# Prompt attention of a two-layer decoder step: alternating the order of TensorE's work between even and odd steps

## The chip, the cores and the metric

The program runs on one core of one Trainium2 chip. Its time is the device time of one execution in microseconds (us), as a median of several runs. The engines of the core work from queues of their own and wait for each other on semaphores: TensorE (PE in the profile, its weight loads PEld), VectorE (DVE), ScalarE (ACT), GpSimd (POOL) and SyncE (SP, which starts transfers).

## What is computed

One inference step of a two-layer decoder: 512 prompt tokens and 8 sample tokens, width 1024, 16 heads of 64 in 4 key/value groups. Layer 0 mixes tokens with native sparse attention (NSA), layer 1 with indexer sparse attention (DSA); each layer has a SwiGLU before and behind its mixer. The part that matters here is prompt attention, in blocks of 128 queries:

```python
# NSA: the selected and the window branch are softmax attention over the tokens
s = jnp.einsum('btkgd,btkmd->btkgm', qr, ks).astype(jnp.float32) * scale
p = masked_softmax(s, smask[:, :, :, None, :])
o_slc = jnp.einsum('btkgm,btkmd->btkgd', p.astype(vs.dtype), vs)
...
return g[..., 0:1] * o_cmp + g[..., 1:2] * o_slc + g[..., 2:3] * o_win
...
# DSA: one branch, over the tokens that the indexer chose
p = masked_softmax(s, valid[:, :, None, None, :])
return jnp.einsum('btkgm,btmkd->btkgd', p.astype(v.dtype), v)
```

All of it is in float32.

## The kernel before

The function attention() runs twice: once for layer 0 (names that begin with nsa_att, two branches and a compressed part) and once for layer 1 (dsa_att, one branch). It works on pairs of heads. A pair in one branch is a round, s = 0, 1, ...: 16 rounds in NSA, 8 in DSA. A round has four steps, one for each block of 128 queries, i = 0 to 3; the steps are numbered through, m = 4s + i. Block i looks at (i+1) x 128 keys. A step goes through these stations:

1. scores(m), on PE, L963: two matmuls on 64 rows each, into one of two banks s_ps (the bank of step m-2, so it waits for max_done of step m-2).
2. maximum(m), on DVE, L1087: adds the mask, finds the row maximum and writes probs; for each of the two heads.
3. exp(m), on ACT, L1044.
4. weigh(m), on DVE, L1093: the reciprocal of the sums. Then POOL, L950, scales probs by it.
5. turn(m), on PE, L981: transposes of 128x128 into one of two banks t_ps: 2 of them for i = 0, 4 for i = 1, 6 for i = 2 (two groups of 3), 8 for i = 3 (two groups of 4). A group waits until the group two before it has been copied out of its bank.
6. copy, out of t_ps into probs_t: on DVE, L1106, for i = 0, 2 and 3; on ACT, L1053, for i = 1.
7. values(s, kc), on PE, L1008, four of them in a round, in the round after it (the last in the one after that). In NSA compressed_values, L998, comes once in two rounds.
8. output, when a pair of heads is done: half on DVE, L1111, half on ACT, L1060.

The order on each engine is written out by loops over m. On PE a step takes scores(m+2), then turn(m-1), then the values that are due. On DVE a step takes weigh(m), maximum(m+2), then a side job if there is one, then the copy of step m-1 (none when i = 2), then the output if one is due (i = 1). On ACT a step takes exp(m+2), then (i = 2) the copy, or (i = 1) the output. Each engine takes its list in this order. The side job is there in DSA alone, in steps 4 to 20: one VectorE instruction in a step (L2536, L2538 in turns, L2534 at the end) that chooses keys for the sample tokens.

Below, S128, S256, S384 and S512 are the scores of i = 0 to 3; T2, T4, T6 and T8 the turns of i = 0 to 3; V with its widths the values, and C the compressed values. In these words PE's order in a round before is: S384 T8 V256, S512 T2 (C), S128 T4 V512, S256 T6 V384+V128.

Of the kernel before, what the change touches and what calls it, by code (L numbers as in the profile page):

```python
# [168 lines left out]
def warm_up(e, pe, out, count):  # L169


    for _ in range(count):
        pe.matmul(out, e.ident_b[:, :], e.causal_b[:, :], start=True, stop=True)
# [698 lines left out]
def attention(e, name, qt, branches, compressed, ot, prefetch, aside=None, prepare=None):  # L872
# [6 lines left out]
    nb = len(branches)  # L879
    S = 8 * nb  # L880
    M = 4 * S
    PT = 2560
    with ExitStack() as ctx:
# [21 lines left out]
        def groups_of(i):  # L905
            return ((0, (0, 1)),) if i == 0 else ((1, (0, 1)),) if i == 1 else ((2 * i - 2, (0,)), (2 * i - 1, (1,)))
# [5 lines left out]
        def block_at(i, kc, par):  # L912

            return kc * P if par == 0 else (i - kc) * P
# [7 lines left out]
        def moving(s, kc, par):  # L922
            at = 384 * kc if par == 0 else 2048 - 512 * kc
            return probs_t[s % 2][:, at + P * kc:at + 512]

        @block.sync
        def _(sp):
            prefetch(sp)
# [24 lines left out]
        @block.tensor  # L953
        def _(pe):
            def scores(m):
                i, b, p = m % 4, m // 4 % nb, m // (4 * nb)
                width, bank = (i + 1) * P, s_ps[m % 2]
                if m >= 2:

                    max_done.wait(pe, 2 * m - 2)  # L960
                for par in range(2):
                    rows = slice(par * HD, (par + 1) * HD)
                    mm = pe.matmul(bank[:, par, 0:width], qt[rows, p, i * P:(i + 1) * P], branches[b].kt[rows, p // 4, 0:width],  # L963
                                   start=True, stop=True)
                mm.then_inc(s_ready.sem, 1)

            def turn(m):
                s, i = m // 4, m % 4
                for g, pars in groups_of(i):
                    if 6 * s + g >= 2:  # L970

                        if g == 3:
                            act_copied.wait(pe, s + 1)
                        else:
                            dve_copied.wait(pe, 5 * s + (-1, 0, 1, 0, 2, 3)[g])
                    scaled.wait(pe, 2 * m + pars[-1] + 1)
                    for par in pars:
                        at = par * (i + 1) * P if len(pars) == 2 else 0
                        for kc in range(i + 1):
                            to = at + block_at(i, kc, par)  # L980
                            mm = pe.transpose(t_ps[g % 2][:, to:to + P], probs[i][par][:, kc * P:(kc + 1) * P], e.ident[:, :])  # L981
                    mm.then_inc(t_ready.sem, 1)

            def o_free(s):
                p = s // nb
                if p >= 2:

                    o_act.wait(pe, p - 1)
                    o_dve.wait(pe, p - 1)

            def compressed_values(s):

                p = s // nb
                p_t, v_bd = compressed
                o_free(s)
                for par in range(2):
                    head = 8 * (p // 4) + 4 * par + p % 4
                    pe.matmul(o_ps[p % 2][par * HD:(par + 1) * HD, :], v_bd[:, head, :], p_t, start=True, stop=False)  # L998

            def values(s, kc):  # L1000
                p, b = s // nb, s % nb
                if kc == 0:
                    act_copied.wait(pe, s + 1)
                    dve_copied.wait(pe, 5 * s + 5)
                    if b == 0 and compressed is None:
                        o_free(s)
                for par in range(2):
                    mm = pe.matmul(o_ps[p % 2][par * HD:(par + 1) * HD, kc * P:512],  # L1008
                                   branches[b].v_of(kc, 2 * (p // 4) + par), moving(s, kc, par),
                                   start=kc == 0 and b == 0 and compressed is None, stop=b == nb - 1 and kc == 2)  # L1010
                if kc == 2:
                    mm.then_inc(pv_done.sem, 1)

            warm_up(e, pe, o_ps[0][:, 0:P], 64)
            scores(0)
            scores(1)
            for m in range(M + 1):
                s, i = m // 4, m % 4
                if m + 2 < M:
                    scores(m + 2)  # L1020
                if m >= 1:
                    turn(m - 1)
                if m >= 5:
                    if i == 1 and (s - 1) % nb == 0 and compressed is not None:
                        compressed_values(s - 1)
                    if i == 2:
                        values(s - 1, 0)
                    if i == 3:
                        values(s - 1, 1)
                        values(s - 1, 3)  # L1030
                if i == 0 and s >= 2:
                    values(s - 2, 2)
            if compressed is not None and (S - 1) % nb == 0:
                compressed_values(S - 1)
            for kc in (0, 1, 3, 2):
                values(S - 1, kc)
# [1786 lines left out]
```

## Time and profile before

| | before |
|---|---|
| median of 3 runs | 2402.17 us (2398.2 to 2403.61) |
| the profiled execution | 2401.8 us, span 2400.0 us |
| busy PE / DVE / ACT / POOL | 95% / 45% / 31% / 14% of the span |
| NSA prompt attention | first scores at 679.25 us, last values done at 827.07 us |
| DSA prompt attention | first scores at 1834.14 us, last values done at 1912.47 us |

The times of the last two lines are read from the timeline of PE. A busy share is of the whole span; the two attention stages are 226 us of it together, and their shares are read by windows. In the timeline, a row gives the start, the duration, the engine, the line and operation, and in brackets how long the engine was idle before it and which engine's work ended that. In float32 each matmul of L963, L1008 and L998 shows as two entries, so "x4" there is two matmuls; a transpose shows as one.

### The profile page before, as it was taken

The page shows a single profiled execution, that of the slowest core. Times are in us where ns is not written, and L with a number is a line of the kernel's source. Part 1 is how long each engine was busy: PE and PEld are TensorE (multiplying, and loading weights), DVE is VectorE, ACT ScalarE, POOL GpSimd, SP SyncE. Part 2 cuts the span into 40 slices and gives each one's busy share as a digit, 9 for nine tenths or more (in the row PEclk, how much of TensorE's full clock was granted, in tenths as well). Part 3 has the DMA queues.
Part 4 walks back from the last instruction along what each step waited for, and adds up shares of the span by engine and source line. Part 5 has one row for each costly group of instructions (what it writes and reads, how often), then busy time and mean ns, then how long its engine had stood idle before and what let it go on. Part 6 is the DMA issues. An engine that isn't in the chain of part 4 may idle for free. (4 is left out here: it accounts for less than half of the span.)

```text
span 2400.0 us, 42964 instructions
## 1 busy us (share of the span) xinstructions
PE 2278.6 (95%) x17146; PEld 2057.5 (86%) x17146; DVE 1081.9 (45%) x1907; ACT 737.5 (31%) x1224; POOL 334.2 (14%) x422
## 2 busy tenths in 40 slices
PE   5999999996899999999999999999998889999997
PEld 5999999775764479999999999999665479999997
DVE  5442443223267644433434442444376735433433
ACT  2221332223146533322222221322255523322221
POOL 1000003100135321000012000003174320000002
PEclk8999999997999999999999999999999989999998
DMA  3332332224430022333232333332213022232331
GB/s 99 96 101 81 90 97 78 82 79 125 159 115 1 27 68 84 95 97 88 87 102 75 95 96 88 89 100 71 79 53 109 1 70 79 88 105 79 87 101 58
DMA packets 328119, 202.53 MB, mean 84 GB/s; under 512 B 11698, under 2 KB 307946, under 8 KB 327962
## 3 DMA queue, kind: packets, MB, share of 16 engines
q1 hardware_dynamic: 323866, 199.19, 27.9%
q10 hardware_dynamic: 4160, 2.10, 0.3%
q8 instruction: 59, 0.97, 0.2%
q14 instruction: 34, 0.28, 0.0%
HBM read 194.74 MB, written 10.70 MB: 86 GB/s over the span
## 5 line engine op out<-in xcount | busy, mean ns | idle before, releaser
L159 DVE TENSOR_TENSOR w_lo<-w_stage,w_hi 128x1024 fp32r<-128x1024 f32 (+1 forms) x268 | 356.4, 1330 | 827.1 <-ACT w_hi L152 827.0
L152 ACT ACTIVATE w_hi<-w_stage 128x1024 fp32r<-128x1024 f32 (+1 forms) x278 | 314.0, 1130 | 751.0 <-PE y_ps L166 344.2
L164 PE MATMUL gate_ps<-h_hi,w_hi 128*128 128x260 f32 x1408 | 402.3, 286 | 17.2 <-DVE h_lo L188 7.5
L165 PE MATMUL gate_ps<-h_lo,w_hi 128*128 128x260 f32 x1408 | 401.1, 285 | 0.0
L166 PE MATMUL gate_ps<-h_hi,w_lo 128*128 128x260 f32 x1408 | 400.3, 284 | 0.0
L164 PE MATMUL up_ps<-h_hi,w_hi 128*128 128x260 f32 x1408 | 398.8, 283 | 0.0
L164 PE MATMUL y_ps<-a_hi,w_hi 128*128 128x260 f32 x1408 | 398.5, 283 | 0.0
L165 PE MATMUL up_ps<-h_lo,w_hi 128*128 128x260 f32 x1408 | 398.1, 283 | 0.0
L165 PE MATMUL y_ps<-a_lo,w_hi 128*128 128x260 f32 x1408 | 398.0, 283 | 0.0
L166 PE MATMUL y_ps<-a_hi,w_lo 128*128 128x260 f32 x1408 | 397.9, 283 | 0.0
L166 PE MATMUL up_ps<-h_hi,w_lo 128*128 128x260 f32 x1408 | 397.4, 282 | 0.0
L164 PEld LDWEIGHTS gate_ps<-h_hi,w_hi 128*128 128x128 f32 x1408 | 268.1, 190 | 19.6 <-issue 15.8
L206 POOL TENSOR_TENSOR sq<-x 128x520 f32<-128x520 f32 x48 | 55.9, 1165 | 1561.6 <-DVE x L446 1110.6
L165 PEld LDWEIGHTS gate_ps<-h_lo,w_hi 128*128 128x128 f32 x1408 | 268.8, 191 | 0.0
L166 PEld LDWEIGHTS gate_ps<-h_hi,w_lo 128*128 128x128 f32 x1408 | 268.8, 191 | 0.0
L165 PEld LDWEIGHTS up_ps<-h_lo,w_hi 128*128 128x128 f32 x1408 | 265.7, 189 | 0.1
L166 PEld LDWEIGHTS up_ps<-h_hi,w_lo 128*128 128x128 f32 x1408 | 265.8, 189 | 0.0
L164 PEld LDWEIGHTS y_ps<-a_hi,w_hi 128*128 128x128 f32 x1408 | 265.6, 189 | 0.0
L166 PEld LDWEIGHTS y_ps<-a_hi,w_lo 128*128 128x128 f32 x1408 | 265.2, 188 | 0.0
L165 PEld LDWEIGHTS y_ps<-a_lo,w_hi 128*128 128x128 f32 x1408 | 265.2, 188 | 0.0
L164 PEld LDWEIGHTS up_ps<-h_hi,w_hi 128*128 128x128 f32 x1408 | 264.9, 188 | 0.1
L364 ACT ACTIVATE a_hi<-act_t 128x520 f32 (+1 forms) x88 | 56.3, 639 | 241.2 <-DVE act_t L427 241.2
(420 smaller groups left out, 3142.4 us busy)
## 6 DMA issues: line engine op xcount, KB each, us to landing
w_stage<-w_ffn_in SPq DMA_DIRECT2D x176, 512.0 KB, 3.7
w_stage<-w_ffn_out SPq DMA_DIRECT2D x64, 704.0 KB, 4.5
w_stage<-w_nsa_in SPq DMA_DIRECT2D x20, 512.0 KB, 3.4
w_stage<-w_dsa_in SPq DMA_DIRECT2D x16, 512.0 KB, 3.6
w_stage<-w_nsa_out SPq DMA_DIRECT2D x8, 512.0 KB, 3.6
cmp_page<-cache_nsa_cmp SPq DMA_DIRECT2D x16, 256.0 KB, 4.3
w_stage<-w_dsa_out SPq DMA_DIRECT2D x8, 512.0 KB, 3.7
nsa_win_s<-state_nsa_win SPq DMA_DIRECT2D x1, 4080.0 KB
```

The lines of the kernel that those rows point to most:

```text
L152: act.activation(e.w_hi[slot][:, 0:cols], e.w_stage[slot][:, 0:cols], ACT.Copy).then_inc(e.hi_done, 1)
L159: dve.tensor_tensor(e.w_lo[slot][:, 0:cols], e.w_stage[slot][:, 0:cols], e.w_hi[slot][:, 0:cols].bitcast(F32), ALU.subtract).then_inc(e.lo ...
L164: pe.matmul(out, w_hi, x_hi, start=first, stop=False)
L165: pe.matmul(out, w_hi, x_lo, start=False, stop=False)
L166: return pe.matmul(out, w_lo, x_hi, start=False, stop=last)
L206: pool.tensor_tensor(e.sq[:, :], e.x[:, i, :], e.x[:, i, :], ALU.mult).then_inc(e.sq_done, 1)
L364: act.activation(a_hi[:, j, :] if isinstance(j, int) else a_hi[:, ds(j, 1), :], act_t[:, :, :], ACT.Copy).then_inc(e.a_hi_done, 1)
```

## The change

The diff touches the loop of PE in attention() alone. In even steps the order stays: scores, turn, values. In odd steps it becomes values, turn, scores. Nothing is added or taken away; no other engine's list is touched, and all waits stay with the instructions that had them.

```diff
             for m in range(M + 1):
                 s, i = m // 4, m % 4
-                if m + 2 < M:
-                    scores(m + 2)
-                if m >= 1:
-                    turn(m - 1)
-                if m >= 5:
-                    if i == 1 and (s - 1) % nb == 0 and compressed is not None:
+                if i % 2 == 0:
+
+                    if m + 2 < M:
+                        scores(m + 2)
+                    if m >= 1:
+                        turn(m - 1)
+                    if i == 2 and s >= 1:
+                        values(s - 1, 0)
+                    if i == 0 and s >= 2:
+                        values(s - 2, 2)
+                else:
+
+                    if i == 1 and s >= 1 and (s - 1) % nb == 0 and compressed is not None:
                         compressed_values(s - 1)
-                    if i == 2:
-                        values(s - 1, 0)
-                    if i == 3:
+                    if i == 3 and s >= 1:
                         values(s - 1, 1)
                         values(s - 1, 3)
-                if i == 0 and s >= 2:
-                    values(s - 2, 2)
+                    turn(m - 1)
+                    if m + 2 < M:
+                        scores(m + 2)
```

PE's list in a round of NSA without compressed values, before, from S384 on (nsa_att_s_ps are scores, nsa_att_t_ps turns, nsa_att_o_ps values):

```order
L963 MATMUL nsa_att_s_ps<-nsa_kt,nsa_qt 128x384 x2
L981 MATMUL nsa_att_t_ps<-const,nsa_att_p 128x128 x8
L1008 MATMUL nsa_att_o_ps<-nsa_att_pt,nsa_z 64x256 x2
L963 MATMUL nsa_att_s_ps<-nsa_kt,nsa_qt 128x512 x2
L981 MATMUL nsa_att_t_ps<-const,nsa_att_p 128x128 x2
L963 MATMUL nsa_att_s_ps<-nsa_kt,nsa_qt 128x128 x2
L981 MATMUL nsa_att_t_ps<-const,nsa_att_p 128x128 x4
L1008 MATMUL nsa_att_o_ps<-nsa_att_pt,nsa_z 64x512 x2
L963 MATMUL nsa_att_s_ps<-nsa_kt,nsa_qt 128x256 x2
L981 MATMUL nsa_att_t_ps<-const,nsa_att_p 128x128 x6
L1008 MATMUL nsa_att_o_ps<-nsa_att_pt,nsa_z 64x384 x2
L1008 MATMUL nsa_att_o_ps<-nsa_att_pt,nsa_z 64x128 x2
```

And PE's list in the same round now:

```order
L963 MATMUL nsa_att_s_ps<-nsa_kt,nsa_qt 128x384 x2
L981 MATMUL nsa_att_t_ps<-const,nsa_att_p 128x128 x8
L1008 MATMUL nsa_att_o_ps<-nsa_att_pt,nsa_z 64x256 x2
L981 MATMUL nsa_att_t_ps<-const,nsa_att_p 128x128 x2
L963 MATMUL nsa_att_s_ps<-nsa_kt,nsa_qt 128x512 x2
L963 MATMUL nsa_att_s_ps<-nsa_kt,nsa_qt 128x128 x2
L981 MATMUL nsa_att_t_ps<-const,nsa_att_p 128x128 x4
L1008 MATMUL nsa_att_o_ps<-nsa_att_pt,nsa_z 64x512 x2
L1008 MATMUL nsa_att_o_ps<-nsa_att_pt,nsa_z 64x384 x2
L1008 MATMUL nsa_att_o_ps<-nsa_att_pt,nsa_z 64x128 x2
L981 MATMUL nsa_att_t_ps<-const,nsa_att_p 128x128 x6
L963 MATMUL nsa_att_s_ps<-nsa_kt,nsa_qt 128x256 x2
```

S512 has moved behind T2 and next to S128; S256 has moved behind T6, to the end of the round and next to the following S384; the values of the fourth step stand next to V512. Neighbours of one kind are more, changes of kind fewer.

PE's list in DSA with its waits, before, around S256 and T6 (dsa_att_s_ps are scores, dsa_att_t_ps turns):

```order
L963 MATMUL dsa_att_s_ps<-dsa_kt,dsa_qt 128x256 [waits max_done]
L963 MATMUL dsa_att_s_ps<-dsa_kt,dsa_qt 128x256
L981 MATMUL dsa_att_t_ps<-const,dsa_att_p 128x128 [waits probs_scaled,dve_copied]
L981 MATMUL dsa_att_t_ps<-const,dsa_att_p 128x128 x2
L981 MATMUL dsa_att_t_ps<-const,dsa_att_p 128x128 [waits probs_scaled,act_copied]
L981 MATMUL dsa_att_t_ps<-const,dsa_att_p 128x128 x2
L1008 MATMUL dsa_att_o_ps<-dsa_att_pt,dsa_z 64x384 x2
L1008 MATMUL dsa_att_o_ps<-dsa_att_pt,dsa_z 64x128 x2
```

And PE's list now, in the same place:

```order
L1008 MATMUL dsa_att_o_ps<-dsa_att_pt,dsa_z 64x384 x2
L1008 MATMUL dsa_att_o_ps<-dsa_att_pt,dsa_z 64x128 x2
L981 MATMUL dsa_att_t_ps<-const,dsa_att_p 128x128 [waits probs_scaled,dve_copied]
L981 MATMUL dsa_att_t_ps<-const,dsa_att_p 128x128 x2
L981 MATMUL dsa_att_t_ps<-const,dsa_att_p 128x128 [waits probs_scaled,act_copied]
L981 MATMUL dsa_att_t_ps<-const,dsa_att_p 128x128 x2
L963 MATMUL dsa_att_s_ps<-dsa_kt,dsa_qt 128x256 [waits max_done]
L963 MATMUL dsa_att_s_ps<-dsa_kt,dsa_qt 128x256
```

S256 now stands behind both groups of T6, the second of which waits for ACT's copy (act_copied).

## Rows read from the trace of the kernel before

**Rows 1.** Windows: start and end, us, busy PE, PEld, DVE, ACT, POOL, clock, DMA.

```profile
740.00:760.00 20.00, 19.76 (x124) 9.49 (x119) 14.86 (x63) 11.29 (x39) 10.42 (x19) 1.00 0.01 2
...
1866.00:1876.00 10.00, 8.69 (x56) 4.18 (x52) 8.74 (x37) 5.85 (x21) 4.12 (x8) 1.00 0.00 0
```

**Rows 2.** Timeline of all engines in NSA: start, duration, engine, line, operation.

```profile
745.80 0.69 DVE L1111 COPY nsa_ot<-nsa_att_o_ps 64x512 f32<-64x512 f32 x1
...
746.65 0.29 DVE L1087 CUSTOM_DVE_ANT_0 nsa_att_p<-nsa_att_s_ps,nsa_att_diagonal 128x128 f32<-128x128 f32 x1
...
746.99 0.40 ACT L1044 ACTIVATE nsa_att_p<-nsa_att_p,nsa_att_neg_max 128x128 f32<-128x128 f32 x1
...
747.40 0.70 PE L963 MATMUL nsa_att_s_ps<-nsa_kt,nsa_qt 64*128 64x256 f32 x4
...
747.77 0.63 ACT L1053 ACTIVATE nsa_att_pt<-nsa_att_t_ps 128x256 f32<-128x256 f32 x2
...
748.15 0.42 DVE L1087 CUSTOM_DVE_ANT_0 nsa_att_p<-nsa_att_s_ps,nsa_att_diagonal 128x256 f32<-128x256 f32 x1 [0.85 <-PE nsa_att_s_ps L963]
...
748.85 1.01 DVE L1106 COPY nsa_att_pt<-nsa_att_t_ps 128x384 f32<-128x384 f32 x2
...
749.78 0.21 DVE L1093 RECIPROCAL nsa_att_weight<-nsa_att_sums 128x1 f32<-128x1 f32 x2
...
749.95 0.92 PE L963 MATMUL nsa_att_s_ps<-nsa_kt,nsa_qt 64*128 64x384 f32 x4
...
750.79 1.09 PE L981 MATMUL nsa_att_t_ps<-const,nsa_att_p 128*128 128x128 f32 x8
750.91 0.56 DVE L1087 CUSTOM_DVE_ANT_0 nsa_att_p<-nsa_att_s_ps,nsa_att_diagonal 128x384 f32<-128x384 f32 x1 [0.92 <-PE nsa_att_s_ps L963]
...
751.82 0.65 PE L1008 MATMUL nsa_att_o_ps<-nsa_att_pt,nsa_z 128*64 128x256 f32 x4
...
751.87 1.28 DVE L1106 COPY nsa_att_pt<-nsa_att_t_ps 128x512 f32<-128x512 f32 x2
...
752.40 1.13 PE L963 MATMUL nsa_att_s_ps<-nsa_kt,nsa_qt 64*128 64x512 f32 x4
...
753.33 1.09 POOL L950 TENSOR_SCALAR nsa_att_p<-nsa_att_p,nsa_att_weight,nsa_gates 128x256 f32<-128x256 f32 x2 [2.42 <-DVE nsa_att_weight L1093]
...
753.46 0.44 PE L981 MATMUL nsa_att_t_ps<-const,nsa_att_p 128*128 128x128 f32 x2
753.58 0.69 DVE L1087 CUSTOM_DVE_ANT_0 nsa_att_p<-nsa_att_s_ps,nsa_att_diagonal 128x512 f32<-128x512 f32 x1 [0.29 <-PE nsa_att_s_ps L963]
...
753.83 0.49 PE L963 MATMUL nsa_att_s_ps<-nsa_kt,nsa_qt 64*128 64x128 f32 x4
...
754.56 0.63 PE L981 MATMUL nsa_att_t_ps<-const,nsa_att_p 128*128 128x128 f32 x4 [0.24 <-POOL nsa_att_p L950]
...
754.80 0.42 DVE L1106 COPY nsa_att_pt<-nsa_att_t_ps 128x256 f32<-128x256 f32 x1
```

**Rows 3.** Timeline of PE in NSA: S256 of the second and of the last round.

```profile
684.26 0.70 PE L963 MATMUL nsa_att_s_ps<-nsa_kt,nsa_qt 64*128 64x256 f32 x4
...
810.93 0.70 PE L963 MATMUL nsa_att_s_ps<-nsa_kt,nsa_qt 64*128 64x256 f32 x4
```

**Rows 4.** Timeline of PE in DSA: S256 of second and last round, and a T6.

```profile
1838.99 0.70 PE L963 MATMUL dsa_att_s_ps<-dsa_kt,dsa_qt 64*128 64x256 f32 x4
...
1868.59 0.55 PE L981 MATMUL dsa_att_t_ps<-const,dsa_att_p 128*128 128x128 f32 x3 [0.55 <-ACT dsa_att_pt L1053]
...
1895.52 0.70 PE L963 MATMUL dsa_att_s_ps<-dsa_kt,dsa_qt 64*128 64x256 f32 x4
```

**Rows 5.** Groups of the side job, 1840 to 1900: busy us, mean ns.

```profile
L2536 DVE MAX8 dsa_is_top<-dsa_is_s 8x8 f32<-8x257 f32 x8 | 3.3, 412 | 0.0
...
L2538 DVE MATCH_REPLACE8 dsa_is_s<-dsa_is_top,dsa_is_s 8x257 f32<-8x257 f32 x8 | 3.2, 400 | 0.0
```

**Rows 6.** Windows, columns as in rows 1, behind the DSA stage.

```profile
1920.00:1930.00 10.00, 5.85 (x55) 2.49 (x54) 2.52 (x8) 1.90 (x7) 0.00 (x0) 0.71 0.00 0
```

## The prediction

> **What bounds the kernel now.** The change is in the two prompt attention stages alone, so I read these, first by windows, then by the timeline of all engines, then by the places where a round begins.
>
> In NSA the windows show PE busy 19.76 of 20 us and DVE 14.86 of 20, at full clock [rows 1]: PE sets the pace. From S256 of the second round to S256 of the last are 14 rounds in 810.93 - 684.26 = 126.67 us [rows 3], 18.10 us for two rounds, one of them with C and an output. In DSA PE is busy 8.69 of 10 us and DVE 8.74 [rows 1]; the six rounds from the second to the last take 1895.52 - 1838.99 = 56.53 us [rows 4]. There neither engine is full, and the second half of a T6 waits 0.55 us for ACT's copy [rows 4]: a chain across engines sets the pace. The reader should see that in NSA, too, DVE has only a quarter of its time to spare, and that it waits for scores before its maxima (0.85, 0.92 and 0.29 us) [rows 2].
>
> **What the change saves.** A change of kind on PE costs a front. T8 takes 1.03 us to the next start and T2 0.37 [rows 2], so a transpose costs 0.11 and the front 0.15. S512 takes 1.06 and S384 0.84 [rows 2]: 0.22 for 128 columns and a front of about 0.18. V256 takes 0.58 [rows 2], of which 0.44 is columns and 0.14 front. A round had 4 fronts of scores, 4 of turns and 3 of values (4 with C); now 2, 4 and 2. Saved: 2 x 0.18 + 0.15 = 0.51 us, with C 0.66. Over 16 rounds of NSA that is 8 x (0.51 + 0.66) = 9.4 us, over 8 of DSA 4.1: at most 13.5 us, if nothing waits.
>
> **What it costs.** DVE's list is as before: weigh(m), maximum(m+2), copy of step m-1. In an odd step PE now gives T before S, but DVE still takes the maximum of that S before the copy of that T. So a T that is done lies in its bank until the S behind it is done and searched, and the T that needs the bank waits. I follow one round of NSA without C from the start of S256, at 0, all durations from rows 2:
>
> - S256 to DVE's start: 748.15 - 747.40 = 0.75. Its two maxima: 0.70 (to 748.85). Sum 1.45.
> - Then both copies of T6: 0.93 (to 749.78). Sum 2.38. T8 needs the first copied: half of 1.01 behind 1.45, and a lag from engine to engine, for which I take POOL's to T4, 754.56 - (753.33 + 1.09) = 0.14: T8 starts at 2.10, where PE was done with S384 at 0.18 + 5 x 0.22 = 1.28. PE waits 0.8.
> - weigh 0.21; the maxima of S384 0.96 (750.91 to 751.87); the first copy of T8, half of 1.28, 0.64, and the lag 0.14: T2 may start at 4.33. PE would be ready at 2.10 + 1.03 + 0.58 = 3.71; it waits 0.62. With C (0.88 of columns more) PE is ready at 4.59 and does not wait.
> - T2 0.37 (753.46 to 753.83), then S512, of which DVE hears 753.58 - 752.40 = 1.18 later. Sum 5.88.
> - Its maxima 1.22 (753.58 to 754.80), the copy of T2 0.42, weigh 0.21. Sum 7.73.
> - The maxima of the next round's S128, long waiting, bring ACT's exp 0.34 later (746.65 to 746.99); the two of them take 0.78 (to 747.77), then ACT copies T4, 0.63, and the lag 0.14. Sum 9.62.
> - Only then can the second half of T6 start: 0.15 + 3 x 0.11 = 0.48. Sum 10.10, and there the next S256 begins.
>
> Beside this, PE ends V384+V128 at about 8.7 and the first half of T6 at about 9.1, so it waits again, 0.5. All that the next lap needs at its start is there, so the lap repeats itself: 10.10 us. In the round with C, T2 comes at 4.59 instead of 4.33, and the output stands on DVE between the copy of T2 and weigh, 0.69 [rows 2]: 11.05. Two rounds are 21.15 us against 18.10, so 14 rounds cost 7 x 3.05 = 21.3 us more. PE's saved fronts are inside this: it is no longer PE's sum that counts.
>
> In DSA each round from the third has an output (0.69), and while the side job lasts DVE takes one instruction of it in each step between maximum and copy, 0.40 or 0.41 [rows 5]; three lie on the lap (behind the maxima of S256, S384 and S512), 1.21. A lap is 10.10 + 0.69 + 1.21 = 12.00. I count the second round without output 11.31, three of 12.00, one in which the job ends 11.5, one without it 10.79: 69.6 us against 56.53, 13.1 more. There is no C.
>
> The first and the last steps lie outside of these laps. The first lap is longer by the same waits (S256 of the second round now comes behind T6, so it starts some 3.5 us later), and of this the last one gives back part, as S256 is now the last of its step. I take 3 us for NSA and 1.5 for DSA, an estimate from the terms of the lap; its bounds are 0 and a full loss of two laps in each stage, 7.5 together.
>
> Sum: 21.3 + 13.1 + 4.5 = 38.9 us. On the profiled execution, 2401.8 us (span 2400.0), that is 2440.7; the median is 0.4 us above that execution: 2441.
>
> What is unsure in it: the lag (0.14; no row for a copy that PE waits for as the last; bounds 0 and 0.24, what T4 stood idle for POOL [rows 2]), how far weigh overlaps with the maxima behind it (up to 0.2 less in a lap), and whether scores directly behind scores pay no front of their own (0.18 more if they do). A lap is good to about 0.5 us, the twenty laps to 10: 2431 to 2451 with the ends as taken, and 2426 to 2454 with their bounds.
>
> **The rivals.**
>
> *The fronts win.* If the copies were out of PE's way, only the saving would be left: 2401.8 - 13.5 = 2388 us, faster. For it: PE is 19.76 of 20 us busy in NSA, and DVE has a quarter free [rows 1]. It decides at one point: the first copy of T6 has to reach PE 1.28 us after the start of S256, and the rows make it 2.10. The 0.8 us would have to come from the 1.45 that DVE spends on the S256 ahead of the copy, which stands ahead of it in DVE's list. DSA, where PE is not full, would give less than its part. The Trainium skill speaks for this rival: TensorEngine Tiling (Array Packing), Key Properties, says that changing the tiling mode drains TensorE, and scores, turns and values are of three modes here. By that rule alone the change can only gain; the fronts above agree with it.
>
> *PE's own two waits, and no lap.* If T8's 0.8 and T2's 0.62 were all, and ACT's copy were in time for T6, two rounds of NSA would cost 0.8 + 0.62 - 0.51 and 0.8 - 0.66, 1.05 together, 8.4 us in the stage, and DSA about nothing: 2410 us. If the waits are shorter still, the two sides cancel: 2398 to 2407, no change. For it: in NSA before, T6 hardly waits. Against it: T6 already waits for ACT in DSA [rows 4], where ACT's place in the chain is the same.
>
> *The clock falls.* PE's own work in a round is 7.9 us (scores and values 20 x 0.22, 20 transposes at 0.11, two fronts at 0.18 and six at 0.15), of 12.0 in DSA: two thirds. Behind the stage, a stretch with PE busy 5.85 of 10 us shows a mean granted clock of 0.71 [rows 6], which is between the two levels of 1.2 and 2.4 GHz. At the lower level PE's work of a round would be 15.7 us, more than the lap: 3.7 us in each of six laps, 22 us, 2463; with NSA too, 14 laps of 5 to 6 us more, 2540. Against it: with PE busy 8.69 of 10 us the clock is full in DSA before [rows 1], and no single wait in the laps above is longer than about 1.3 us. The skill's page TensorE: Matmul & The Clock Gate, Part 4, says that transposes do not count as work for the clock in the same way; a third of this stage's work is transposes, and the full clock of before does not show such an effect.
>
> *The order is not changed.* The lists of PE show that it is, in both stages; no chance.
>
> **How the numbers follow.** My lap: 0.74. PE's own waits alone, 2410: 0.08. They cancel: 0.06. The fronts win: 0.06. The clock falls: 0.06. The predicted time is that of the lap, 2441. The range takes in the lap with its bounds, 2426 to 2454, some room on both sides for a term that I have not seen, and the case of PE's own waits: 2410 to 2462, 0.81 in all. A measurement of this kernel can tell about 0.2% from no change, 5 us: faster 0.06, same 0.06, slower 0.74 + 0.08 + 0.06 = 0.88.
>
> **What the profile of the changed kernel would show.** Right: in NSA, PE busy some 16 of 20 us instead of 19.76; T8 waiting for DVE's copies by about 0.8 us, T2 by about 0.6 in rounds without C, the second half of T6 for ACT's copy; S256 to S256 in turns of about 10.1 and 11.0 us; in DSA 12.0, falling to 10.8 behind the side job; DVE waiting for S256 and S512 a microsecond or more, with a finished T in its bank. The clock full in both stages. Wrong: PE still at 19.7 of 20 us and two rounds under 18 us (the fronts win); T6 going through without a wait for ACT (the lap doesn't close); a granted clock under 1 in the stage.

## The result and the profile after

The changed kernel takes **2437.43 us** (median, 2434.88 to 2442.51), the kernel before 2401.23 us beside it on the same chip: a ratio of 1.0154, with a 95% interval of 1.0132 to 1.0176. It is 36.2 us slower; 2441 was predicted. The profiled execution is the longest one, 2442.51 us (span 2440.7). Some 5 us of it lie between the two stages, where the code is unchanged. The windows from 25 to 45 us behind the end of the NSA stage, in the columns of [rows 1], show where: before, here, and in the run e4 below.

```profile
852.07:872.07 20.00, 16.83 (x149) 14.70 (x142) 9.03 (x16) 7.43 (x15) 1.67 (x2) 0.91 0.27 80
875.35:895.35 20.00, 16.83 (x123) 12.33 (x116) 8.59 (x16) 7.44 (x15) 0.00 (x0) 0.67 0.18 54
850.20:870.20 20.00, 16.82 (x123) 12.41 (x116) 8.53 (x16) 7.44 (x15) 0.00 (x0) 0.66 0.18 54
```

TensorE's granted clock is 0.67 there where it was 0.91; by the clock alone that is 20 x 0.24 = 4.8 us, an estimate. e4 has PE's order of before and shows the low clock too, so these 5 us do not go with PE's order.

The two stages hold the rest of this execution's loss. NSA prompt attention runs from 679.76 to 850.35 us, 170.6 us instead of 147.8; DSA from 1862.43 to 1954.17, 91.7 instead of 78.3. That is 22.8 and 13.4 us, 36.2 together.

First the windows, in the columns of [rows 1]. They answer to the two rows there.

```profile
740.00:760.00 20.00, 16.84 (x104) 8.99 (x106) 13.06 (x55) 10.44 (x37) 9.16 (x16) 1.00 0.00 0
1900.00:1910.00 10.00, 7.25 (x50) 3.81 (x46) 7.31 (x32) 5.29 (x18) 3.84 (x8) 1.00 0.00 0
```

PE is busy 16.84 of 20 us where it was 19.76, at full clock, and DVE, ACT and POOL have all lost busy time as well. No engine is full: something that runs across them sets the pace.

Next the timeline of all engines over one lap of NSA without C, from one S256 to the next (a bracket gives the idle time of the engine ahead of the row, and whose work ended it). It answers to [rows 2].

```profile
741.85 1.35 PE L963 MATMUL nsa_att_s_ps<-nsa_kt,nsa_qt 64*128 64x256 f32 x8
742.60 0.42 DVE L1093 CUSTOM_DVE_ANT_0 nsa_att_p<-nsa_att_s_ps,nsa_att_diagonal 128x256 f32<-128x256 f32 x1 [2.39 <-PE nsa_att_s_ps L963]
...
743.29 1.02 DVE L1112 COPY nsa_att_pt<-nsa_att_t_ps 128x384 f32<-128x384 f32 x2
...
743.90 1.12 PE L981 MATMUL nsa_att_t_ps<-const,nsa_att_p 128*128 128x128 f32 x8 [0.70 <-DVE nsa_att_pt L1112]
...
745.30 1.28 DVE L1112 COPY nsa_att_pt<-nsa_att_t_ps 128x512 f32<-128x512 f32 x2
...
746.04 0.44 PE L981 MATMUL nsa_att_t_ps<-const,nsa_att_p 128*128 128x128 f32 x2 [0.44 <-DVE nsa_att_pt L1112]
...
746.41 1.35 PE L963 MATMUL nsa_att_s_ps<-nsa_kt,nsa_qt 64*128 64x512 f32 x8
...
747.59 0.69 DVE L1093 CUSTOM_DVE_ANT_0 nsa_att_p<-nsa_att_s_ps,nsa_att_diagonal 128x512 f32<-128x512 f32 x1 [0.88 <-PE nsa_att_s_ps L963]
...
748.55 1.94 PE L1008 MATMUL nsa_att_o_ps<-nsa_att_pt,nsa_z 128*64 128x512 f32 x12
...
748.82 0.42 DVE L1112 COPY nsa_att_pt<-nsa_att_t_ps 128x256 f32<-128x256 f32 x1
...
749.75 0.39 ACT L1050 ACTIVATE nsa_att_p<-nsa_att_p,nsa_att_neg_max 128x128 f32<-128x128 f32 x1
...
750.52 0.63 ACT L1059 ACTIVATE nsa_att_pt<-nsa_att_t_ps 128x256 f32<-128x256 f32 x2
...
751.21 0.55 PE L981 MATMUL nsa_att_t_ps<-const,nsa_att_p 128*128 128x128 f32 x3 [0.23 <-ACT nsa_att_pt L1059]
751.68 0.49 PE L963 MATMUL nsa_att_s_ps<-nsa_kt,nsa_qt 64*128 64x256 f32 x2
```

The lines of DVE and ACT have moved by six: the maxima are L1093 here (L1087 before), DVE's copies L1112, exp L1050, ACT's copy L1059. Read the rows downwards as one chain. DVE has nothing to do for 2.39 us, since the next thing in its list is the maximum of S256; the T6 that PE turned ahead of S256 lies finished in its bank. The scores come, DVE searches them, and only then takes the copy (743.29). Neighbours of one kind share a row: the first row is S256 with S384, 746.41 is S512 with S128, 748.55 is V512 with V384+V128; the last row is cut off by the end of the view. T8 needs the bank and starts at 743.90, after 0.70 us idle. Its own copy comes behind the maxima of S384, and T2 waits 0.44 us for the first half of it. S512 stands behind T2; DVE waits 0.88 us for S512 and then does its maxima, T2's copy, weigh and the maxima of S128; ACT makes exp of S128, then copies T4 (750.52); the second half of T6 waits for that copy, and the next S256 stands behind T6.

The waits, grouped (us in total, times, longest), are of 690 to 845 in NSA.

```profile
DVE nsa_att_p L1093 <- PE nsa_att_s_ps L963: 53.5, 30, 3.3
...
PE nsa_att_t_ps L981 <- DVE nsa_att_pt L1112: 12.9, 21, 0.7
...
PE nsa_att_t_ps L981 <- ACT nsa_att_pt L1059: 4.9, 14, 0.5
```

T8 and T2 wait for DVE's copies 21 times, once for each T8 and in the rounds without C for T2 too; the second half of T6 waits for ACT in each of 14 laps. DVE in turn waits 53.5 us for scores. PE and DVE wait for each other by turns.

### The profile page after: what moved, and what is told of

Same layout as the page of the kernel before. It is cut to its first block and busy times, and to the rows that moved or that the text cites. A ratio compares the mean times of both kernels' runs of the same rounds, so it can differ in the third digit from the quotient of the medians.

```text
span 2440.7 us, 42964 instructions
## 1 busy us (share of the span) xinstructions
PE 2279.1 (93%) x17146; PEld 2067.1 (85%) x17146; DVE 1081.9 (44%) x1907; ACT 738.7 (30%) x1224; POOL 335.1 (14%) x422
```

## Experiments

**The theory** is the lap: scores come behind a turn on PE, while DVE's list still has the maximum of those scores ahead of the copy of that turn; the bank comes free late, and the wait closes into a lap through DVE, PE and ACT. **Rivals**: the scores are late in themselves, whatever DVE does; it is only PE's own waits; the saved fronts are not real. Laps below are from S256 to S256 in the timeline of PE; in NSA those without and with C, from the third round on. Each time has the ratio to the kernel before, on the same chip, with its 95% interval. The last column is the length of the two stages together in the profiled execution. The code between the stages is the same in all runs, but takes from 1006.5 to 1012.1 us in these executions, so a few us of difference are better read from the stages than from the whole.

| run | us | ratio | NSA laps | DSA laps | stages |
|---|---|---|---|---|---|
| before | 2401 | 1 | 8.6 to 8.9 / 9.46 | 8.7 to 10.0 | 226.2 |
| changed kernel | 2437.4 | 1.0154 [1.0132, 1.0176] | 9.83 / 10.9 to 11.0 | 10.6 to 11.8 | 262.3 |
| e1_copy_first | 2413.5 | 1.0055 [1.004, 1.007] | 8.90 / 9.9 to 10.1 | 9.2 to 10.5 | 236.2 |
| e2_copies_first | 2399.1 | 0.9996 [0.9984, 1.0007] | 8.45 / 9.4 to 9.5 | 8.8 to 10.0 | 226.4 |
| e3_outputs_later | 2388.2 | 0.9948 [0.9933, 0.9964] | 8.44 / 8.67 | 8.3 to 9.3 | 217.0 |
| e4_lists_alone | 2394.8 | 0.9974 [0.9964, 0.9984] | 8.64 / 9.51 | 8.5 to 9.1 | 221.2 |
| e5_step1 | 2429.8 | 1.0126 [1.0105, 1.0146] | 9.59, then 10.3 to 12.0 / 9.69 | 9.9 to 12.3 | 257.6 |
| e6_step3 | 2417.6 | 1.0071 [1.0054, 1.0087] | 9.38 / 9.81 | 9.5 to 10.8 | 239.1 |
| e7_values_only | 2391.9 | 0.9965 [0.9954, 0.9976] | 8.63 / 9.35 | 8.5 to 9.0 | 218.3 |
| e8_act_copy_first | 2423.8 | 1.0097 [1.0076, 1.0118] | 9.45 / 10.5 to 10.7 | 10.0 to 11.2 | 250.7 |
| e9_values_and_lists | 2393.7 | 0.9965 [0.9955, 0.9975] | 8.63 / 9.36 | 8.2 to 8.8 | 216.7 |

**e1_copy_first: only DVE's list follows.** The changed kernel, with DVE taking the copy ahead of the maximum in odd steps. PE gives scores as late as in the change.

```diff
+                if m >= 1 and i % 2 == 1:
+                    copy(m - 1)
                 if m + 2 < M:
                     maximum(m + 2)
...
-                if m >= 1 and i != 2:
+                if m >= 1 and i == 0:
                     copy(m - 1)
```

> The changed kernel, and on VectorE in odd steps the copy of the turn now stands ahead of the maxima of the scores behind it. PE's list stays that of the change, so its scores come as late as there. My theory (the copy stands behind a maximum whose scores come after the turn, so finished turns block their bank): T8 no longer waits for VectorE (0.7 us before), a lap of NSA falls from 9.83 and 10.91 us to about 9.2 and 10.1, a lap of DSA with side job and output from 11.7 to about 10.7; about 2418 us, between before and the change, since ACT's copy behind two exps still holds T6. Rival A (it is the lateness of the scores themselves: the chain from scores over maximum, exp and scaling to the turn is now too short): laps stay near 9.8 and 10.9, about 2435 us. Rival B (more changes of shape or colder weights on TensorE itself): nothing changes either, 2437 us.

Measured 2413.5 us: 24 of the 36 us are back, 4.5 us better than expected. In the timeline of PE, T8 now starts right behind S256 and S384 (1.28 us after the start of S256, as on paper without a wait), while ACT's copy still holds T6:

```profile
724.43 1.35 PE L963 MATMUL nsa_att_s_ps<-nsa_kt,nsa_qt 64*128 64x256 f32 x8
725.71 1.10 PE L981 MATMUL nsa_att_t_ps<-const,nsa_att_p 128*128 128x128 f32 x8
...
734.09 0.55 PE L981 MATMUL nsa_att_t_ps<-const,nsa_att_p 128*128 128x128 f32 x3 [0.71 <-ACT nsa_att_pt L1059]
```

Late scores as such are therefore not the cause: their place in PE's list is the same here. The place of the copy in DVE's list is two thirds of the loss. The Trainium skill says, in PSUM — Partial Sum Buffer, Engine vs sequencer instructions, that the queues of ScalarE, VectorE and GpSimd are strict FIFO; this run agrees, since the same instructions in another order on DVE are worth 24 us.

**e8_act_copy_first: only ACT's list follows.** The changed kernel, with ACT copying T4 ahead of its exp.

```diff
+                if i == 2:
+                    copy(s)
                 if m + 2 < M:
                     exp(m + 2)
-                if i == 2:
-                    copy(s)
```

> The changed kernel with only ScalarE's copy of T4 ahead of the exp in its step; VectorE's list is as before. My theory: the second half of T6 no longer waits for ScalarE, but POOL's scaling of the same turn, which stands behind the same late weigh, ends 0.3 us earlier than that copy only; a lap falls by 0.3 to 0.5 us, 20 laps by 6 to 10: about 2429 us. If ScalarE's copy alone were the cause of the cost (rival): near 2405.

Measured 2423.8 us, 13.6 less than the change where 6 to 10 were forecast. Each lap of NSA behind the first whole one is shorter by 0.36 to 0.38 us, as forecast; those of DSA by 0.53 to 0.57, more than forecast. In NSA that is less than the 0.78 of the two exps, because T6 then waits for the next in line, POOL's scaling of its probs; and T8's wait for DVE is what it was:

```profile
746.57 1.12 PE L981 MATMUL nsa_att_t_ps<-const,nsa_att_p 128*128 128x128 f32 x8 [0.71 <-DVE nsa_att_pt L1112]
...
753.96 1.16 PE L981 MATMUL nsa_att_t_ps<-const,nsa_att_p 128*128 128x128 f32 x6 [0.71 <-POOL nsa_att_p L950]
```

So ACT's copy is a part of the lap, in NSA in the size that was given to it, and the lap stays closed without it.

**e2_copies_first: both lists follow.** e1 and e8 together.

> As the one with VectorE's copy first, and on ScalarE the copy of T4 now stands ahead of the exp in its step. My theory: the second half of T6 no longer waits for an exp of the next round; a lap of NSA falls to about 8.4 (without compressed values) and 9.3 us (with, where the outputs still lie on the chain), one of DSA to about 9.9; about 2398 us, even with before or a little faster. Rival A (late scores): still 2430 us or more.

Measured 2399.1 us, the time of the kernel before. What e1 and e8 remove is the whole loss. The saved fronts are in this time too, so some waiting must still be left.

**e3_outputs_later: and the outputs out of the way.** e2, and DVE and ACT take the output one step later, in the step in which DVE has no copy to take (the same edit on both engines).

```diff
-                if i == 1 and s >= 2 and (s - 1) % nb == 0:
+                if i == 2 and s >= 2 and (s - 1) % nb == 0:
                     output((s - 1) // nb - 1)
```

> As the one with both copies first, and both outputs now stand one step later (i = 2, where VectorE has no copy, and behind ScalarE's exp). My theory: all terms that I found on the lap are off it; laps of NSA of about 8.3 and 8.75 us against 18.10 for two before, of DSA about 9.2 against 9.4 on average before; about 2388 us, faster than before, since now the saved fronts of TensorE show (at most 13.5 us). Rival A: 2430 us or more. If it is no faster than before: the fronts are not saved, or VectorE is the bound.

Measured 2388.2 us, as expected. This version beats both kernels, by 0.5% over the one before. What is left is seen in PE's timeline, one place of NSA and one of DSA:

```profile
746.25 1.09 PE L981 MATMUL nsa_att_t_ps<-const,nsa_att_p 128*128 128x128 f32 x8
747.27 0.65 PE L1008 MATMUL nsa_att_o_ps<-nsa_att_pt,nsa_z 128*64 128x256 f32 x4
748.23 0.44 PE L981 MATMUL nsa_att_t_ps<-const,nsa_att_p 128*128 128x128 f32 x2 [0.31 <-DVE nsa_att_pt L1112]
...
1859.78 0.44 PE L981 MATMUL dsa_att_t_ps<-const,dsa_att_p 128*128 128x128 f32 x2 [1.06 <-DVE dsa_att_pt L1112]
```

T2 comes soon after T8 in the new order and needs T8's copy: 0.31 us of waiting in NSA rounds without C, and 1.06 in DSA while the side job is on DVE (0.31 behind it).

**e4_lists_alone: the lists without the change.** The kernel before, with DVE's and ACT's lists of e3. It tells what PE's order is worth by itself.

> The kernel before, with its order on TensorE, and VectorE's and ScalarE's lists as in the version with copies first and outputs later. It tells how much of that version's gain is due to these lists alone. My theory: NSA is bound by TensorE before, so its two rounds stay near 18.1 us (17.9 at best, the waits of T4 for POOL), and DSA gains some tenths of a microsecond in a round where T6 waited for ScalarE; about 2397 us. If it is as fast as that version, TensorE's new order gives nothing even when it doesn't have to wait.

Measured 2394.8 us: the lists alone are worth 0.26%. Between e4 and e3 only PE's order differs, and the new one is 6.6 us better by the medians. In NSA a pair of laps is 17.11 us instead of 18.15, 1.04 saved of the 1.17 that the fronts of [rows 2] promise. In DSA six laps take 53.9 us instead of 52.9: nothing is saved there, and the waits of T2 shown above fit that, since the last lap, without the side job, is shorter in the new order (8.28 against 8.52). Of the lists' own gain most lies in DSA: six laps take 52.9 us where the kernel before took 56.5.

**e5_step1 and e6_step3: half of the change each.** Only the steps of i = 1 (C, T2, S512), or only those of i = 3 (values, T6, S256), are in the new order.

```diff
-                if i % 2 == 0:
+                if i != 1:
...
+                    if i == 3 and s >= 1:
+                        values(s - 1, 1)
+                        values(s - 1, 3)
```

> Half of the change: only the steps with i = 1 take values, turn, scores (S512 behind T2, next to S128); the steps with i = 3 take S256, T6, V384+V128 as before. My theory, by the terms of the lap: S512 can't start before T2, and T2 waits for the first copy of T8, so the chain S384, maxima, copy, T2, S512, maxima, copy of T2, exp, ACT's copy, T6 still closes, without S256 in it: laps of NSA of about 9.3 (no compressed values) and 10.5 us, of DSA up to 10.8; about 2420 us, most of the cost. Rival (each half costs its part evenly): about 2419 as well, and the other half the same; the lap tells them apart by the other half, which should cost less. Rival (one half is free): 2400.

And e6, where C moves back behind T2 as before:

```diff
-                if i % 2 == 0:
+                if i != 3:
...
+                    if i == 1 and s >= 1 and (s - 1) % nb == 0 and compressed is not None:
+                        compressed_values(s - 1)
                     if i == 2 and s >= 1:
                         values(s - 1, 0)
```

> The other half: only the steps with i = 3 take values, turn, scores (S256 behind T6, next to S384); the steps with i = 1 take S512, T2, compressed values as before. My theory: T8 waits for the copy of T6 behind the maxima of S256 (about 0.7 us), but S512 waits for no turn, so only part of the lap is left: about 9.0 and 9.7 us in NSA, 10.5 in DSA with side job; about 2411 us, less than the half with i = 1.

Measured 2429.8 and 2417.6 us. Each half costs by itself, 29 and 17 us, and the two don't add: 46 would be the sum, 36 is the whole. Each lengthens the laps by a wait of its own: in NSA T8 waits 0.7 us for DVE in e6, the second half of T6 0.47 us for ACT in e5. But both were forecast too low, e5 by 10 us and e6 by 7. In e5 the long lap of a pair is also not the one with C, as was forecast, but the one behind it, in which T6 waits for POOL. A larger cause is in the rows: at some laps PE's work itself is slow. PE's timeline behind a T6 that waited (the laps there are 11.8 instead of 10.3):

```profile
713.10 0.52 PE L981 MATMUL nsa_att_t_ps<-const,nsa_att_p 128*128 128x128 f32 x3 [0.94 <-POOL nsa_att_p L950]
714.09 0.55 PE L981 MATMUL nsa_att_t_ps<-const,nsa_att_p 128*128 128x128 f32 x3 [0.47 <-ACT nsa_att_pt L1062]
714.57 1.85 PE L1008 MATMUL nsa_att_o_ps<-nsa_att_pt,nsa_z 128*64 128x384 f32 x8
716.34 1.65 PE L963 MATMUL nsa_att_s_ps<-nsa_kt,nsa_qt 64*128 64x384 f32 x4
```

And the windows of the same place, in the columns of [rows 1]:

```profile
711.00:714.00 3.00, 1.67 (x11) 0.61 (x7) 2.89 (x17) 2.87 (x12) 1.71 (x3) 1.00 0.00 0
714.00:718.00 4.00, 3.91 (x16) 1.58 (x17) 0.90 (x4) 1.01 (x5) 1.97 (x4) 0.59 0.01 2
718.00:720.00 2.00, 1.95 (x14) 1.26 (x14) 1.96 (x6) 1.31 (x4) 0.00 (x0) 0.96 0.00 0
```

S384 takes 1.65 us where it took 0.92 [rows 2]: the granted clock fell to its lower level behind 3 us in which PE worked 1.67. It makes two laps of NSA 11.81 and 12.02 us where their like take 10.3 or 10.4. The clock falls so four times in NSA and three in DSA; at some 1.6 us each that would be up to 11 us, an estimate near the miss of 10. The laps without it are 20.0 to 20.1 us a pair, against 19.8 forecast. In e6 the clock falls once in NSA; there a pair of laps is 19.19 us against 18.7 forecast, 3.4 us in seven pairs and about half of the miss. Which term was too small, and what the rest is, stays open.

**e7_values_only: the values ahead of the turn, the scores left first.** PE's odd steps are scores, values, turn; DVE and ACT as in the change.

```diff
                 else:
 
+                    if m + 2 < M:
+                        scores(m + 2)
...
                     turn(m - 1)
-                    if m + 2 < M:
-                        scores(m + 2)
```

> In odd steps scores come first again, and only values and turn are exchanged: scores, values, turn. My theory (the scores behind the turn are what costs): TensorE has as many fronts as before (11 in a round), scores are as early as before, and T6 comes 1 us later than before, which its wait for ScalarE's copy had partly taken anyway: about 2400 us, within 5 of before. Rival (turns behind values are what costs): over 2415 us.

Measured 2391.9 us, 8.5 us faster than before: a miss of the expectation, which had taken the values' move for nearly neutral. In DSA it is not, as PE's timeline there shows:

```profile
1860.56 0.70 PE L963 MATMUL dsa_att_s_ps<-dsa_kt,dsa_qt 64*128 64x256 f32 x4
1861.19 1.08 PE L1008 MATMUL dsa_att_o_ps<-dsa_att_pt,dsa_z 128*64 128x384 f32 x8
1862.21 1.04 PE L981 MATMUL dsa_att_t_ps<-const,dsa_att_p 128*128 128x128 f32 x6
```

Before, T6 stood right behind S256, and its second half waited 0.55 us for ACT's copy [rows 4]. In other rounds the same 0.55 us is put down to POOL's scaling, which ends within 0.1 us of that copy. One of them, in PE's timeline of the kernel before:

```profile
1878.43 0.55 PE L981 MATMUL dsa_att_t_ps<-const,dsa_att_p 128*128 128x128 f32 x3 [0.55 <-POOL dsa_att_p L950]
```

In e7 V384+V128 fills that time, whichever of the two ends last, and T6 goes through whole. The last four laps of DSA fall from 9.4 to 10.0 us to 8.5 to 9.0. With DVE's and ACT's lists as they are, the harm of the change thus lies in the scores behind the turn, and the move of the values is a gain. With the lists moved as well, scores behind the turn are no harm (e3).

**e9_values_and_lists: are the two gains to be added?** e7's order on PE, with ACT's copy first and both outputs later as in e3; on ACT:

```diff
+                if i == 2:
+                    copy(s)
                 if m + 2 < M:
                     exp(m + 2)
-                if i == 2:
-                    copy(s)
-                if i == 1 and s >= 2 and (s - 1) % nb == 0:
+                if i == 2 and s >= 2 and (s - 1) % nb == 0:
                     output((s - 1) // nb - 1)
```

> Scores, values, turn in odd steps, as in the run where only values and turn are exchanged, and besides: ScalarE's copy of T4 ahead of the exp in its step, both outputs one step later; VectorE takes its maxima ahead of its copies as before. TensorE is full there in NSA (rounds of 8.63 and 9.35 us) and nearly so in DSA (8.8), so I expect little more: about 2390 us, no faster than the version with TensorE's order of the change and both copies first (2388). If it falls to 2384 or less, waits on ScalarE were left, and scores first is the better order with the lists mended.

Measured 2393.7 us, the same ratio as e7. In the whole time the lists add nothing to e7 that can be told, and the laps of NSA are the same to 0.01 us: in DSA the values had already covered the wait of T6. The profiled executions say a little more: the two stages are 1.6 us shorter than in e7, and the unchanged code between them 5.0 us longer (1011.4 against 1006.5). e3 keeps the lowest median, but its interval overlaps those of e7 and e9, and by the stages alone e9 is even with it.

## Why the prediction was right, and where it was off

**What bounds, and where the end is set.** Right. PE went from 19.76 to 16.84 of 20 us (some 16 was said), and a chain across the engines took its place.

**The savings.** They are real and of the size that was read: S256 and S384 now stand in one row, and where nothing waits T8 follows 1.28 us behind its start (e1), which is five times 0.22 and one front; and e3 against e4 gives 1.04 of 1.17 us for two rounds of NSA. The "fronts win" rival, 2388 us, is just what e3 measures once DVE and ACT follow, though not by the same sum, so that the number agrees by luck: e3's lists are worth part of it, and in DSA the fronts give nothing. In the change itself the first copy of T6 reached PE at 2.05 and not at 1.28, so the rival fell at the point that was named for it. The rule on draining at a change of mode (the Trainium skill, TensorEngine Tiling (Array Packing), Key Properties) fits the fronts; alone it would have had the sign wrong, because PE was not what the new order was limited by.

**The lap, term by term.** From the rows above, as time since S256:

| point of the lap | predicted | measured |
|---|---|---|
| T8 starts | 2.10 | 743.90 - 741.85 = 2.05 |
| T2 starts | 4.33 | 746.04 - 741.85 = 4.19 |
| DVE has S512 | 5.88 | 5.74 |
| copy of T2 | 7.10 | 6.97 |
| ACT copies T4 | 8.85 | 8.67 |
| second half of T6 | 9.62 | 9.36 |
| next S256 | 10.10 | 9.83 |

Each station is there in its order. The 0.27 us too much lie in small terms. The lag was taken as 0.14 three times; from DVE's copy to PE it was 0.10 (743.29 + 0.51 to 743.90, twice), from ACT's copy 0.06 (750.52 + 0.63 to 751.21). And instructions of DVE in a row overlap by some 0.1, named among the unsure terms. In rounds with C it was 10.91 or 11.04 against 11.05. PE's timeline gives the whole stage, from S256 of the second to that of the last round, as in [rows 3]:

```profile
688.62 2.51 PE L963 MATMUL nsa_att_s_ps<-nsa_kt,nsa_qt 64*128 64x256 f32 x8
...
834.88 1.35 PE L963 MATMUL nsa_att_s_ps<-nsa_kt,nsa_qt 64*128 64x256 f32 x8
```

146.26 us for 14 laps instead of 126.67: 19.6 us more, 21.3 predicted.

**DSA.** The same two rows are 1870.85 and 1939.30: 68.45 us instead of 56.53, 11.9 more where 13.1 was predicted, with laps of 11.6 to 11.8 under the side job (12.00 predicted) and 10.55 behind it (10.79). The first of them, without output, took 11.60 where 11.31 was predicted: a fall of the clock lies in it (below). One reading of the kernel before was narrower than it looked: of the waits of T6's second half in DSA, [rows 4] shows one for ACT's copy, but POOL's scaling ends at about the same time, so the rows before do not tell which of the two holds T6. In the changed kernel ACT's copy does hold it: with that copy first (e8) the laps of DSA fall by 0.53 to 0.57 us.

```profile
1870.85 1.35 PE L963 MATMUL dsa_att_s_ps<-dsa_kt,dsa_qt 64*128 64x256 f32 x8
...
1939.30 1.35 PE L963 MATMUL dsa_att_s_ps<-dsa_kt,dsa_qt 64*128 64x256 f32 x8
```

**The ends of the stages.** 22.8 - 19.6 = 3.2 in NSA and 13.4 - 11.9 = 1.5 in DSA, against 3 and 1.5. So by parts the laps were 31.5 us for 34.4 predicted, and the ends 4.7 for 4.5.

**PE's own waits and no lap; cancelling.** Fell: the second half of T6 waits for ACT in all 14 laps, which closes the lap, and each half of the change costs alone (e5, e6).

**The clock: the step that was partly wrong.** "The clock full in both stages" holds for nearly all of them, not for their first lap, and a granted clock under 1 in the stage was named as a sign of being wrong. PE's timeline and the windows of NSA's beginning:

```profile
686.80 0.52 PE L981 MATMUL nsa_att_t_ps<-const,nsa_att_p 128*128 128x128 f32 x3 [1.87 <-POOL nsa_att_p L950]
...
685.00:686.00 1.00, 0.00 (x0) 0.00 (x0) 1.00 (x6) 1.00 (x3) 0.01 (x1) 1.00 0.79 229
686.00:687.00 1.00, 0.20 (x2) 0.23 (x3) 0.60 (x6) 1.00 (x5) 1.00 (x2) 1.00 0.84 277
687.00:690.00 3.00, 2.53 (x12) 1.77 (x12) 0.11 (x1) 0.73 (x4) 1.80 (x3) 0.56 0.74 219
690.00:693.00 3.00, 2.93 (x12) 1.57 (x8) 3.00 (x13) 1.86 (x7) 0.88 (x2) 0.50 0.84 240
693.00:695.00 2.00, 2.00 (x9) 0.52 (x8) 1.02 (x4) 0.54 (x2) 0.94 (x2) 0.71 0.75 252
```

PE did 0.20 us of work in two microseconds, as T6 waited 1.87 us for POOL; then the clock was at its lower level, 0.50, for about 7 us, and S256 with S384 of the second round (688.62 above) took 2.51 us instead of 1.35. The prediction said that no single wait in the laps is longer than about 1.3 us. That is so, but it left out the ends of the stages, where it prices a longer start, and in one lap the clock fell all the same. The first NSA lap is 11.63 us, 0.7 over its like. DSA shows a shorter fall from 1875 to 1879, in the lap of 11.60 us, behind a wait of T2 of 1.33 us. These two cost some 1 us together, an estimate from the two laps, not the 22 us and more of the rival in which the clock falls for good. So the two errors, the lags and the clock, partly cancel in the sum.

## What to carry to other kernels

An order on one engine is half of a pairing: when a producer is moved behind another instruction, look in the in-order list of the engine that reads it for work on the other that must now wait, and move that list in the same edit; here moving the lists of DVE and ACT turned 36 us lost into 12 gained, of which these lists alone give 5 (e4). Write one lap out with rows from the trace and follow it until it comes back to its start, since a wait that closes into a lap is paid in each round; here half of the edit cost 29 of the 36 us. In front of a turn that waits for another engine's copy, put work that needs nothing from it, as the values do in e7.

## What the runs showed of the hardware that was not expected

The granted clock can fall inside a stage that is busy on the whole: in e5 behind 3 us with PE busy 1.67, with no single idle time over 0.94 us among the rows shown, to 0.59 of full over the next 4 us. The kernel e6 has about the same busy share in NSA (17.75 of 20 us in 740 to 760; e5 17.74) and one short dip in that stage where e5 has four, so the share alone doesn't tell which kernel falls. The Trainium skill describes in TensorE: Matmul & The Clock Gate, A second HAM failure mode: psum-queue depth-cycling, a kernel whose short idle times between groups of matmuls made the clock swing; e5 agrees with it in that the idle times shown ahead of the fall are short, 0.94 and 0.47 us. What separates e5 from e6 is open: no run here varies that alone.

The clock behind a stage can hide a gain within it. Over the same unchanged 20 us of work behind NSA it is 0.91 in the kernel before and in e7, and 0.66 or 0.67 in e4 and in the changed kernel; the whole code between the stages differs by 5 us with it.
